# A streaming encoder step on one core: the first two input panels computed step by step while x is still being transposed

## The reference, cut to what matters

```python
def rmsnorm(x, g):
    y = xf * lax.rsqrt(jnp.mean(xf * xf, axis=-1, keepdims=True) + EPS)
    return (y * g).astype(x.dtype)
qa, ka, va, qb, kb, vb, gates = jnp.split(rmsnorm(x, g_norm1) @ w_in, SPLITS, axis=-1)
oa = swa(qa, ka, va, rel_bias_table, sinks)       # sliding window, relative bias
ob = stick_breaking(qb, kb, vb)
x = x + (g[..., :D] * (oa @ w_proj_a) + g[..., D:] * (ob @ w_proj_b)) @ w_out
x = x + square(relu(rmsnorm(x, g_norm2) @ w_up)) @ w_down
```

## Time and profile before

| | |
|---|---|
| median of 3 runs | 863.22 us (862.98 to 863.53) |
| the profiled execution's own time | 863.73 us |
| its span, first to last instruction | 861.9 us |
| busy: TensorE matmul, VectorE, ScalarE, GpSimd | 97%, 74%, 44%, 34% |
| mean granted clock of TensorE | 0.991 |

### The profile page before, as it was taken

The page is one execution under the profiler, slowest core; times in us unless marked ns, Lnnn a source line. Parts: engine busy times, 40 slices in busy tenths (PEclk is TensorE's granted clock), DMA queues, the critical chain, the costliest instruction groups (busy, mean ns, idle before and its releaser), DMA issues.

```text
span 861.9 us, 15995 instructions
## 1 busy us (share of the span) xinstructions
PE 832.4 (97%) x6197; PEld 812.0 (94%) x6197; DVE 641.1 (74%) x1103; ACT 383.2 (44%) x638; POOL 294.9 (34%) x213
## 2 busy tenths in 40 slices
PE   6999999999999999999999999999999999999994
PEld 4999999999899989899999999999999999999994
DVE  5778887344698898968335889479884889488995
ACT  5545666142457686653343333333332333333431
POOL 2553222311644455425434500443016400552330
PEclk9999999999999999999999999999999999999997
DMA  7761210632111111223321311431133312422203
GB/s 220 241 194 57 65 61 20 205 122 87 50 51 49 49 49 49 70 86 150 123 89 59 98 49 55 143 98 53 56 101 133 97 49 89 127 76 82 64 1 110
DMA packets 67392, 78.17 MB, mean 91 GB/s; under 512 B 2520, under 2 KB 62992, under 8 KB 66960
## 3 DMA queue, kind: packets, MB, share of 16 engines
q1 hardware_dynamic: 66912, 76.40, 27.8%
q10 hardware_dynamic: 432, 1.11, 0.3%
HBM read 70.15 MB, written 8.93 MB: 92 GB/s over the span
## 4 chain that ended last, share of the span: by engine, by line
PE 86%; DVE 10%; issue 1%; ACT 1%; DMA 1%; ACTq 0%; DVEq 0%
PE pan L1429 55%; PE pan L1607 13%; PE att L1607 11%; PE att L1471 1%; PE att L1545 1%; DVE sp_lo L1087 1%; DVE sp L1081 1%; PE att L1518 1%; DVE sp_hi L1085 1%; DVE sp L1076 1%; PE att L1535 1%; DMA x_rows<-in_x_prompt 1%; DVE sp_lo L1150 1%; PE att L1685 1%; DVE m_a L1115 0%
## 5 line engine op out<-in xcount | busy, mean ns | idle before, releaser
L438 POOL TENSOR_TENSOR w_lo<-raw,w_hi 128x512 fp32r<-128x512 f32 x164 | 226.8, 1408 | 459.8 <-ACT w_hi L759 182.3
L1429 PE MATMUL pan<-a_hi,w_hi 128*128 128x288 f32 x672 | 146.5, 300 | 0.0
L1429 PE MATMUL pan<-a_lo,w_hi 128*128 128x288 f32 x672 | 144.5, 297 | 0.0
L1429 PE MATMUL pan<-a_hi,w_lo 128*128 128x288 f32 x672 | 144.5, 297 | 0.0
L1429 PE MATMUL pan<-h_hi,w_hi 128*128 128x288 f32 x512 | 110.0, 296 | 0.0
L1429 PE MATMUL pan<-h_hi,w_lo 128*128 128x288 f32 x512 | 109.7, 295 | 0.0
L1429 PE MATMUL pan<-h_lo,w_hi 128*128 128x288 f32 x512 | 109.7, 295 | 0.0
L1429 PEld LDWEIGHTS pan<-a_hi,w_hi 128*128 128x128 f32 x672 | 108.2, 190 | 1.6 <-POOL w_lo L438 1.3
L1429 PEld LDWEIGHTS pan<-a_hi,w_lo 128*128 128x128 f32 x672 | 108.9, 190 | 0.0
L1429 PEld LDWEIGHTS pan<-a_lo,w_hi 128*128 128x128 f32 x672 | 108.7, 190 | 0.0
L1607 PE MATMUL pan<-F_hi,w_hi 128*128 128x288 f32 x320 | 95.4, 298 | 0.0
(11 more groups left out here) (244 smaller groups left out, 1737.2 us busy)
## 6 DMA issues: line engine op xcount, KB each, us to landing
raw<-in_w_in SPq DMA_DIRECT2D x34, 512.0 KB, 4.8
raw<-in_w_up SPq DMA_DIRECT2D x32, 512.0 KB, 4.7
raw<-in_w_down SPq DMA_DIRECT2D x32, 512.0 KB, 4.7
raw<-in_w_out SPq DMA_DIRECT2D x8, 512.0 KB, 4.1
x_spill<-xT SPq DMA_DIRECT2D x1, 2304.0 KB, 11.3
xT<-x_spill SPq DMA_DIRECT2D x1, 2304.0 KB, 10.8
x_rows<-in_x_prompt SPq DMA_DIRECT2D x2, 1024.0 KB, 6.9
raw<-in_w_pa SPq DMA_DIRECT2D x4, 512.0 KB, 4.5
```

The lines of the kernel that those rows point to most:

```text
L438: last = nc.gpsimd.tensor_tensor(w_lo[:, slot, k:k + 4, :], raw[:, rs, k:k + 4, j * P:(j + 1) * P], w_hi[:, slot, k:k + 4, :].bitcast(F32) ...
L1429: got = nc.tensor.matmul(out[:, h, 0:HALF], w, x[:, h * HALF:(h + 1) * HALF], start=first and n == 0, stop=last and n == 2)
```

## The change

- Loading: x comes in four column quarters of 512 KB with a semaphore each; SyncE's order is quarter 0, sample rows, first weights k 0 to 3, quarters 1 and 2, first weights k 4 to 7, quarter 3, the next two weight loads (no longer behind a wait), then the constants. g1 and g2 move to ScalarE's queue ahead of `ident`.
- TensorE begins with 24 matmuls of zeros (128x256, bf16) whose result is not used.
- The prompt part of a block k is transposed into one of three PSUM banks, and `a_hi` and `a_lo` are formed straight from PSUM. `xT` is copied off by VectorE or, for k = 1 and 3, ScalarE, behind that. The 64 sample columns of all k are transposed at once into bank 3, scaled, rounded and subtracted in three instructions.
- Panels 0 and 1 are computed together: step k multiplies both panels' high weights with `a_hi` and `a_lo` (8 matmuls), with the transposes of block k+3 behind it. The low weights' 32 matmuls follow in a block. The bias table's product stands behind step 6.
- Panel 2 goes to PSUM banks 2 and 3, with `spread_rms` in its middle.
- The first weights are rounded in two instructions of 128x1024 that span both panels; the five squares follow one another, behind the `frow` copy and the rounding of panel 2's weights; panel 3's are rounded behind the root.

```diff
--- before
+++ after
@@ -242,6 +247,17 @@
             return att[:, 2 * pair:2 * pair + 2, :].rearrange("p b n -> p (b n)")[:, 0:TOK]
+        ACT_X = (1, 3)
+        DVE_X = tuple(k for k in range(KT) if k not in ACT_X)
+        def x_bank(k):
+            return att[:, k % 3, :]
+        def landed(slot, count):
...
@@ -320,24 +336,33 @@
                 v = w.rearrange("(k p) n -> p k n", p=P)
                 return lambda h: v[:, :, c * 512 + 256 * h:c * 512 + 256 * h + 256]
-            for part in range(2):
-                cols = slice(part * D // 2, (part + 1) * D // 2)
-                sp_.dma_start(x_rows[:, 0:TT, cols], x_prompt.rearrange("(t p) d -> p t d", p=P)[:, :, cols]).then_inc(x_in[part], 16)
-                if part == 0:
-                    sp_.dma_start(grow[0:KT, :], g1.rearrange("(k p) -> k p", p=P)).then_inc(grow_in, 16)
-                    sp_.dma_start(grow[KT:2 * KT, :], g2.rearrange("(k p) -> k p", p=P)).then_inc(grow_in, 16)
-                    sp_.dma_start(x_rows[0:NEW, TT, :], x_sample).then_inc(xs_in, 16)
-            load(0, 0, wide(w_in, 2), None)
+            def x_piece(q):
+                cols = slice(q * 2 * P, (q + 1) * 2 * P)
+                sp_.dma_start(x_rows[:, 0:TT, cols], x_prompt.rearrange("(t p) d -> p t d", p=P)[:, :, cols]).then_inc(x_in[q], 16)
+            def first_weights(h):
+                sp_.dma_start(raw[:, 0, 4 * h:4 * h + 4, :], wide(w_in, 2)(h)).then_inc(w_first[h], 16)
+            x_piece(0)
+            sp_.dma_start(x_rows[0:NEW, TT, :], x_sample).then_inc(xs_in, 16)
+            first_weights(0)
+            x_piece(1)
+            x_piece(2)
+            first_weights(1)
+            x_piece(3)
+            load(1, 1, wide(w_in, 0), None)
             sp_.dma_start(nsink[:], sinks.unsqueeze(0).to_broadcast([P, SWH])).then_inc(const_in, 16)
             sp_.dma_start(table[:], rel_table).then_inc(const_in, 16)
             sp_.dma_start(oneh[:], onehot).then_inc(const_in, 16)
             sp_.dma_start(cst[:], consts[:, P:]).then_inc(const_in, 16)
-            sp_.wait_ge(x_in[1], 16)
-            load(1, 1, wide(w_in, 0), None)
             load(0, 2, wide(w_in, 1), 2)
             sp_.dma_start(ckaR[:], cache_swa_k).then_inc(ca_in, 16)
-            sp_.wait_ge(xT_ready, KT)
+            sp_.wait_ge(xT_ready, len(DVE_X))
+            sp_.wait_ge(xa_ready, len(ACT_X))
+            sp_.wait_ge(xs_ready, 1)
             sp_.dma_start(x_spill, xT[:]).then_inc(spilled, 16)
             sp_.wait_ge(frow_ready, 1)
             sp_.dma_start(rel_rows, frow[:]).then_inc(rows_out, 16)
@@ -439,8 +464,13 @@
                                                    w_hi[:, slot, k:k + 4, :].bitcast(F32), ALU.subtract)
                 last.then_inc(w_lo_ready, 1)
-            split(0, 0, 0, 1)
-            split(1, 0, 1, 2)
+            for h in range(2):
+                pool.wait_ge(w_hi_ready, h + 1)
+                for j in range(2):
+                    low = nc.gpsimd.tensor_tensor(w_lo[:, j, 4 * h:4 * h + 4, :], raw[:, 0, 4 * h:4 * h + 4, j * P:(j + 1) * P],
+                                                  w_hi[:, j, 4 * h:4 * h + 4, :].bitcast(F32), ALU.subtract)
+                    if h:
+                        low.then_inc(w_lo_ready, 1)
...
@@ -520,6 +550,8 @@
                 round_w(first_panel(b) + 4 + j, j, b + 2 + (j // 2))
+            act.dma_start(grow[0:KT, :], g1.rearrange("(k p) -> k p", p=P)).then_inc(grow_in, 16)
+            act.dma_start(grow[KT:2 * KT, :], g2.rearrange("(k p) -> k p", p=P)).then_inc(grow_in, 16)
             act.dma_start(ident[:], consts[:, 0:P]).then_inc(ident_in, 16)
             act.preload_act_table(ACT.Sqrt)
             act.wait_ge(zero_ready, 1)
@@ -528,34 +560,44 @@
             def squares(n, t):
                 w = width(t)
-                if t == TT:
+                if n == 0:
                     act.wait_ge(xs_in, 16)
-                elif t == 0:
-                    act.wait_ge(x_in[0], 16)
-                    act.wait_ge(x_in[1], 16)
+                elif n == 1:
+                    for q in range(4):
+                        act.wait_ge(x_in[q], 16)
                 if n:
                     act.wait_ge(ss_ready, n)
                 nc.scalar.activation(junk[0:w, :], x_rows[0:w, t, :], ACT.Square, accum_out=ss[0:w, t:t + 1]).then_inc(ss_ready, 1)
+            def round_first(h):
+                act.wait_ge(w_first[h], 16)
+                nc.scalar.activation(w_hi[:, 0:2, 4 * h:4 * h + 4, :], raw[:, 0, 4 * h:4 * h + 4, :].rearrange("p k (j n) -> p j k n", j=2),
+                                     ACT.Copy).then_inc(w_hi_ready, 1)
             for k in range(KT):
-                act.wait_ge(xT_ready, k + 1)
-                nc.scalar.activation(a_hi[:, k, :], xT[:, k, :], ACT.Copy, scale=gcol[:, k:k + 1]).then_inc(h_hi_ready, 1)
-                if k in (1, 4, 6, 7):
-                    n = (1, 4, 6, 7).index(k)
-                    squares(n, (TT, 0, 1, 2)[n])
-                if k in (3, 5):
-                    act.wait_ge(raw_in[0], 32)
-                    j = (k - 3) // 2
-                    nc.scalar.activation(w_hi[:, j, :, :], raw[:, 0, :, j * P:(j + 1) * P], ACT.Copy).then_inc(w_hi_ready, 1)
-            squares(4, 3)
+                act.wait_ge(xT_out, k + 1)
+                nc.scalar.activation(a_hi[:, k, 0:SEQ], x_bank(k), ACT.Copy, scale=gcol[:, k:k + 1]).then_inc(h_hi_ready, 1)
+                if k in ACT_X:
+                    nc.scalar.activation(xT[:, k, 0:SEQ], x_bank(k), ACT.Copy).then_inc(xa_ready, 1)
+                if k == 0:
+                    act.wait_ge(xs_scaled, 1)
+                    nc.scalar.activation(a_hi[:, :, SEQ:TOK], xs_g[:], ACT.Copy).then_inc(xs_hi, 1)
+                    round_first(0)
+                elif k == 4:
+                    nc.scalar.activation(xT[:, :, SEQ:TOK], att[:, 3, :].rearrange("p (k n) -> p k n", k=KT), ACT.Copy).then_inc(xs_ready, 1)
+                elif k == 2:
+                    round_first(1)
+            act.wait_ge(frow_out, 1)
+            nc.scalar.activation(frow[:], att[0:SWH, 3, 0:RELS], ACT.Copy).then_inc(frow_ready, 1)
+            act.wait_ge(raw_in[1], 32)
+            nc.scalar.activation(w_hi[:, 2, :, :], raw[:, 1, :, 0:P], ACT.Copy).then_inc(w_hi_ready, 1)
+            for n, t in enumerate((TT, 0, 1, 2, 3)):
+                squares(n, t)
             act.wait_ge(mean_ready, 1)
             nc.scalar.activation(rtok[:, 0:TT + 1], ss[:, 0:TT + 1], ACT.Sqrt).then_inc(root_ready, 1)
+            nc.scalar.activation(w_hi[:, 3, :, :], raw[:, 1, :, P:2 * P], ACT.Copy).then_inc(w_hi_ready, 1)
             act.preload_act_table_set("natural_log_exp_and_others")
-            act.wait_ge(frow_out, 1)
-            nc.scalar.activation(frow[:], pan[0:SWH, 1, 0, 0:RELS], ACT.Copy).then_inc(frow_ready, 1)
-            act.wait_ge(raw_in[1], 32)
-            for j in range(2):
-                nc.scalar.activation(w_hi[:, 2 + j, :, :], raw[:, 1, :, j * P:(j + 1) * P], ACT.Copy).then_inc(w_hi_ready, 1)
             def qa_high(f):
                 act.wait_ge(tile_taken, 2 * (2 + f) + 2)
...
@@ -855,23 +898,28 @@
                     nc.vector.tensor_copy(smask[:, h * NEW:(h + 1) * NEW], cst[:, 2 * P:2 * P + NEW])
                 nc.vector.tensor_scalar(nsink[:], nsink[:], -1.0, None, ALU.mult).then_inc(consts_ready, 1)
-            def h_low(k):
+            def take_x(k):
+                nc.vector.tensor_copy(xT[:, k, 0:SEQ], x_bank(k)).then_inc(xT_ready, 1)
+            dve.wait_ge(gcol_out, 1)
+            nc.vector.tensor_copy(gcol[:], pan[:, 1, 1, 0:2 * KT]).then_inc(gcol_ready, 1)
+            dve.wait_ge(gcol_ready, 1)
+            dve.wait_ge(xs_out, 1)
+            nc.vector.tensor_tensor(xs_g[:], att[:, 3, :].rearrange("p (k n) -> p k n", k=KT), gcol[:, 0:KT].unsqueeze(2).to_broadcast([P, KT, NEW]),
+                                    ALU.mult).then_inc(xs_scaled, 1)
+            dve.wait_ge(xs_hi, 1)
+            nc.vector.tensor_tensor(a_lo[:, :, SEQ:TOK], xs_g[:], a_hi[:, :, SEQ:TOK].bitcast(F32), ALU.subtract).then_inc(hs_ready, 1)
+            for k in range(KT):
+                if k in ACT_X:
+                    dve.wait_ge(xa_ready, ACT_X.index(k) + 1)
                 dve.wait_ge(h_hi_ready, k + 1)
-                dve.wait_ge(xT_ready, k + 1)
-                nc.vector.scalar_tensor_tensor(out=a_lo[:, k, :], in0=xT[:, k, :], scalar=gcol[:, k:k + 1],
-                                               in1=a_hi[:, k, :].bitcast(F32), op0=ALU.mult, op1=ALU.subtract).then_inc(h_ready, 1)
-            for k in range(KT):
-                dve.wait_ge(xT_out, k + 1)
-                nc.vector.tensor_copy(xT[:, k, :], att_wide(k % 2)).then_inc(xT_ready, 1)
-                if k == 0:
-                    dve.wait_ge(gcol_out, 1)
-                    nc.vector.tensor_copy(gcol[:], pan[:, 1, 1, 0:2 * KT]).then_inc(gcol_ready, 1)
-                    dve.wait_ge(gcol_ready, 1)
-                if k:
```

(89 more changed lines are left out.)

19 lines of the change are left out of this document (12 added, 7 removed).

## The result

| | before | changed |
|---|---|---|
| median, first comparison (4 runs each) | 863.38 us (862.98 to 864.43) | 858.17 us (855.10 to 859.34) |
| changed / before | | 0.9931 (0.9909 to 0.9952) |
| profiled execution, span | 863.73, 861.9 | 855.1, 853.2 |

Two later comparisons of the same kernel gave 858.42 us, ratio 0.9945 (0.9926 to 0.9964), and 859.15 us, ratio 0.9949 (0.9934 to 0.9964).

A forecast was written before the change was run, and what follows sets the result against it. TensorE, busy 97% of the span, was taken to bound the kernel. Its V transposes moving from 42.22 to 39.7 gave 2.5 us, less 0.1 for small waits: 863.73 to 861.3 us, range 859.2 to 864.8.

The forecast's parts named there:

- The gate: Start of the V transposes on TensorE, behind panel 2; claimed to move from 42.22 to 39.7 us.
- VectorE's second take: VectorE's `take_qkv` behind `constants()`; put at 0.75 us and claimed to be what TensorE waits for at the gate.
- the gain is 42.22 less the new gate: Nothing behind the V transposes is edited, so their earlier start is the whole gain: 2.5 us, 2.4 after small waits.
- step 0: First step of panels 0 and 1 together on TensorE; claimed to start at 10.4 us, about 12.5 with slow transposes.
- steps and table: Steps 0 to 6 and the bias table's product: 11.6 us at 2.4 GHz, plus 1.8 for low clock.
- The clock: TensorE's clock expected low again at step 0, for 3.7 us at half rate, costing 1.8 us.
- the rival in which the zero matmuls keep it high: No half rate in the steps: gate at 37.9, 859.4 us; the two faster rivals together had chance 0.22.
- The rival in which it stays low until the low block: TensorE at 1.2 GHz from step 0 until the low weights' matmuls: gate at 49.5, 871 us; chance 0.14.
- Landings: Arrival of loads at the start: `ident` at 5.5 us, quarter 1 of x at 9.6, each ahead of its use.
- the samples' chain: Before step 0: sample columns transposed, scaled (0.7 us), rounded (0.7), then `a_lo` (0.7); samples out at 7.4 us.
- Squares, chain and takes: From the table product's end: squares 7.2 us, `rrep` 9.3, first take 12.3, `constants()` 2.8, second take 0.75; gate 15.9 behind.
- the spread: `spread_rms` on TensorE in the middle of panel 2; `rrep` claimed to come 0.6 us after TensorE asks for it.

The follow-up runs named there:

- before_zeros: The kernel before with only the memset, semaphore and 24 matmuls of zeros added; 863.28 us, ratio 0.9989 against the kernel before.
- consts_later: The changed kernel with `constants()` moved behind VectorE's second take; 861.03 us, ratio 0.9960 against the kernel before.
- squares_early: The changed kernel with the squares under steps 4 to 7, ahead of the `frow` copy, and the spread in front of panel 2; 860.8 us, ratio 0.9958.

## Why the prediction was wrong

*The gate, right, but its agreement partly luck.* TensorE waits there for VectorE's second take in all five traces, as forecast. The step "the gain is 42.22 less the new gate", taken as a mean over executions, gives 2.25 us by the nine traces; the forecast had 2.4 to 2.5, and gate 39.7 against a mean of 39.75. The single gates lie between 38.02 and 41.17, and terms cancel: step 0 came at 11.8 on average (10.4 forecast), while steps and table took 12.2 us in the first trace and 11.7 in the third, where the clock never fell (13.4 and 11.6 forecast).

*The clock, right in kind.* Low again for 3.4 us of the steps in the first trace (3.7 were taken), low from 7.2 to 17.4 us in the second and fourth, from 8.9 to 15.7 in the fifth. In the third it never fell: that was the rival in which the zero matmuls keep it high, with a gate of 38.0 (37.9 forecast). The rival in which it stays low until the low block occurred in no trace. The early transposes behind the zero matmuls were quick in three of five; with that and the landing of `ident`, step 0 varied from 10.77 to 12.86. The Trainium skill's rule that transposes don't count ("TensorE: Matmul & The Clock Gate", Part 4) agrees with before_zeros, where nothing of the warm start was left in panel 0; but in the third trace the granted clock stayed at 1.00 from 6.0 to 10.7 us, across transposes and waits alone, so the rule alone does not forecast a fall.

*Landings, two wrong.* `ident` was put at 5.5 us and called covered. It landed at 5.8 to 7.4 in the five traces, last of all that the first transposes need, and TensorE waited for it in four of them (0.68 us in the first, 2.31 in the second); before, issued first on its queue, it landed at 3.3 to 4.5. Quarter 1 of x was put at 9.6, ahead of its use. It landed at 10.0 to 10.3, and TensorE waited 1.75 us for it in the first trace and 2.25 in the third: there it was this load and not the samples' chain that ended the last wait before step 0, though in the first trace the chain's `a_lo` was done only 0.15 us before step 0 started.

*Squares, chain and takes, right in the first trace.* 7.3 us from the table product's end to the last square (7.2 taken), `rrep` at 9.4 (9.3), a wait of 0.77 at the spread (0.6), VectorE's second take the last at the gate. `constants()` took 2.1 for 2.8, with one of its passes lengthened beside GpSimd (35.66, 1.22 us) and not two. One row of the steps was wrong: VectorE's passes were called quicker than a step, and in the third trace step 3 waited 0.80 us for one. Panels 4 and 5 found their takes ready, and consts_later shows by how little.

*The step that failed* is the sentence "nothing behind the gate is edited, so the gain is 42.22 less the new gate", used as the whole sum. Timed, the kernel gains 4.7 to 5.4 us, of which the traces find 2.25 at the gate. In one execution the unedited 790 us are 783.5 to 790.1 long: with all nine traces set side by side, each low-clock stretch that one has and another has not (near 180, 205, 320 or 360) costs 1.3 to 1.6 us, each meeting in which the third `sp_lo` pass is held up by GpSimd 1.1, the spacing of matmuls up to 2. The range was built from the terms of the first 40 us alone and had nothing for these.

*What stays open.* Why the changed kernel's mean is lower behind the gate too, by some 2 us. Where it is lower, the nine traces do show. Between the first scores and the last matmul they have 2.75 low-clock stretches of 3.4 us on average before and 1.6 in the changed kernel, which at 1.3 to 1.6 us each is some 1.7 us; meetings that went VectorE's way give 0.6; the spacing of matmuls takes back 0.4. The timed runs agree that such stretches are what varies: among the 27 runs of the changed kernel, and among 117 of the kernel before, an execution whose mean granted clock is 0.001 lower is 0.8 us longer. What is open is why the changed kernel meets fewer of them. Refuted are a fixed shorter length (theory B, as it was put) and the simple form of theory C.

Left are chance in nine traces (1.8 with an error of 1.2), and a milder dependence on the moment: 27 unused matmuls cost 5.4 us and 13 cost 2.4 to 3.1 in the changed kernel, above their 3.8 and 2.0, while 13 cost 1.4 in the kernel before, below it. Each of these differs from one for one by about as much as two medians of twelve runs can. For the milder dependence speaks the clock of consts_later and squares_early, whose first scores came no later in their traces than the changed kernel's: 0.9866 and 0.9869 on average over twelve runs each, against 0.9884 over the 27, which at the price above is 1.2 to 1.5 us of what they lost.

## What to carry to other kernels

Find the point behind which nothing changes, and ask separately how long the rest is in another execution: further traces of the kernel before, compared with the first, would have given a width (787.7 to 790.1 us behind the first scores in four) that this range lacked. Work moved off the critical engine should be followed until all that hangs on it is served: here the squares, put behind other work, made VectorE the last at the gate, and each repair moved the wait to the next take. A small load that everything waits for is better first on its queue: by the landings of `ident` that looks worth up to 2 us in an execution, but no kernel here tested it.
